# First four weight units loaded among the input chunks and split by ScalarE and VectorE, bias table's products behind them

## The chip, the cores and the metric

One core of one Trainium2 chip. The metric is the device time of one execution in microseconds (us); of the kernel before there are three runs, 3272.82 to 3274.39 us, median 3274.05. Engines in the profile: PE (TensorE matmul), PEld (its weight loads), DVE (VectorE), ACT (ScalarE), POOL (GpSimd), SP (SyncE, which here only issues DMAs).

## The reference, cut to what matters

Two stacks of two layers each run over one sequence of 512 positions with 1024 features. The change touches the first stack's first projections and a table that the second stack's attention reads much later:

```python
h = x @ w_in[l]
(fq, fk, fv, fgate, cq, ckv, kr, ...) = jnp.split(h, points, axis=-1)
log_f = jax.nn.log_sigmoid(fgate + fox_b_f[l]); cum = jnp.cumsum(log_f, axis=1)
...
q = _rmsnorm(cq, g_q) @ w_uq;  kv = _rmsnorm(ckv, g_kv) @ w_ukv;  k_rope = _rope(kr, cos, sin)
...
bias = rel_bias[t5_bucket(jnp.maximum(dist, 0))]        # second stack: (Q_BLOCK, S, 8)
logits = einsum('bqhmd,bkhmd->bhmqk', q, k) + bias
```

Everything is float32. The kernel gets float32 products from the faster fp32r matmuls by splitting every operand in a rounded part (`hi`) and the rest (`lo = x - hi`) and adding three products: hi*hi, lo*hi, hi*lo.

## The kernel before, in words

**Weights.** All weights lie in HBM as 516 units of 128 x 1024 floats (512 KB), in the order in which they are used. They pass through four slots: SP loads a unit into `raw[:, u]`, POOL makes `w_hi[:, u]` (a cast, L464) and `w_lo[:, u]` (a subtraction, L466), and PE uses it. SP may load a slot again when POOL has split what lay there (`w_split`), POOL may split into it again when PE has used it (`w_used`). A tiny add on `zero` (L463) stands at the head of every unit. Both engines run this as one loop "stream" of 129 rounds of four units. The first units are `kr` (the gate and the rotary key), `c0`, `c1` (the latent queries), `fk0`; then `c2`, `fq0`, `fq1`, `fk1`, `fv0`, `fv1`, `uq`.

**Input.** `x` comes in eight chunks of 128 x 512 (256 KB) into `resid`: even ones are issued by SP ahead of the weights (L440), odd ones by ACT (L1316). ACT makes `xn_hi` (L1093) and DVE `xn_lo` (L1509), in halves of 256 positions: first the eight first halves, then the eight second ones.

**Start of PE.** PE begins with 24 small products (L994, L995) that spread the 32 relative-position biases over distances: four score banks `bank_s` and the two `bank_a`. DVE prepares their operands (L1890 to L1902) and copies the four score banks to `t5_row` (L1912), ACT copies the other two (`copy_bank(("t5", n)...)`) and sends `t5_row` to HBM (L1333). ACT then waits for that transfer (`t5_out`, L1336) before it issues the loads of `par1`, `rope` and the `alibi` table (into `mla_v`), since `rope` and the table lie where `t5_row` lay.

**First projections.** `project_halves` runs the four first units over the chunks, half by half: `kr` and `c0` on chunk n, `c1` and `fk0` on chunk n-3 (`LN_LAG`), three matmuls of 256 columns each, 192 in all. PE reaches the first matmul of `c1` and of `fk0` at n = 3. `project` then does `c2` and `fq0` (24 matmuls of 512 columns each). After them PE waits for `added` of `("lat", "pair")`, the sum of the squares of `c0` and `c1`, and takes two token sums (L533), then `fq1`, `fk1`, the spread of the two norms (L541), and `fv` (`project_rows`), which needs both `bank_v`.

**DVE and ACT beside it.** DVE works strictly in this order: fills of `aug_q` and `aug_k` (L1917 to L1921), the wait for `rope` and the table (`par_in.after("tables1")`, L1922), the four operations that read the `kr` bank and finish the rotary key (L1926 to L1934), the copy of `fk0` (L1754), and the sum `("lat", "pair")` (L1528). ACT copies each latent bank and squares it (`latent(n)`).

Of the kernel before, what the change touches and what calls it, by code (L numbers as in the profile page):

```python
# [22 lines left out]
F32 = mybir.dt.float32  # L23
F32R = mybir.dt.float32r
ALU = mybir.AluOpType
ACT = mybir.ActivationFunctionType
# [5 lines left out]
S = 512  # L32
# [49 lines left out]
TURN_LAG = 2  # L82

# [197 lines left out]
def build(nc, t, known):  # L281
# [3 lines left out]
    with ExitStack() as ctx:  # L285
# [123 lines left out]
        act_step = signal("act_step")  # L409

# [26 lines left out]
        @block.sync  # L437
        def _(sp):
            for c in range(0, DC, 2):
                sp.dma_start(resid[:, c, :], t["x"][:, c, :]).then_inc(*x_in[c].done("x", 16))  # L440
            with loop(sp, "stream", UNITS // SLOTS) as i:
                for u in range(SLOTS):
                    sp.wait_ge(*w_split.before(("unit", u)))
                    sp.dma_start(raw[:, u, :], t["w_stream"][i, u]
                                 ).then_inc(*raw_in[u].done("unit", 16))
            for c in range(0, DC, 2):
                sp.wait_ge(*scaled.after(("final", c + 1)))
                sp.dma_start(t["out"][:, c:c + 2, :], resid[:, c:c + 2, :]).then_inc(*out_done.done(("out", c), 16))
            sp.wait_ge(*out_done.after(("out", DC - 2)))


        @block.gpsimd
        def _(pool):
            pool.sem_inc(w_split.sem, SLOTS)
            pool.memset(zero[:, :], 0.0).then_inc(*fills.done("zero"))
            pool.memset(ones[:, :], 1.0).then_inc(*fills.done("ones"))
            pool.wait_ge(*fills.after("ones"))
# [13 lines left out]
        def _(pe):  # L471
# [225 lines left out]
            def ffn_halves(tag):  # L697

                project_halves([[((tag, "gate0", k), a_bank), ((tag, "up0", k), v_bank)] for k in range(2)],
                               lambda c, s: x_lo.after(("ln2", c, s)), LN_LAG, *late_half("ln2", "layer1", DEPTH - 1))  # L700
                project((tag, "gate1", 0), a_bank)
                project((tag, "up1", 0), v_bank,
                        inside={4: lambda: square_sums("rms1", added.after(("first", DC - 1)), ln_sum[:, :])})
                project((tag, "gate1", 1), a_bank, inside={2: lambda: spread("rms1")})
                project((tag, "up1", 1), v_bank)
                ffn_rest(tag, 2)
                down(tag, None, 2)

# [278 lines left out]
            pe.wait_ge(*rel_in.after("bucket_of"))  # L987
            pe.wait_ge(*dve_step.after("rel_lo"))
            rows = slice(0, BUCKETS + 1)
            for n in range(6):  # L990
                b = bank_s[n] if n < 4 else a_bank(("t5", n))
                for m, at, cut in t5_parts(n):
                    out = b[:, at:at + cut.stop - cut.start]
                    pe.matmul(out, rel_hi[rows, m, :], bucket_r[rows, cut], start=True, stop=False)  # L994
                    mm = pe.matmul(out, rel_lo[rows, m, :], bucket_r[rows, cut], start=False, stop=True)  # L995
                mm.then_inc(*sums.done(("t5", n)))
# [88 lines left out]
        def _(act):  # L1085
# [233 lines left out]
            for s in range(2):  # L1319
                for c in range(DC):  # L1320
                    act.wait_ge(*x_in[c].after("x"))
                    split_hi_half("in1", c, s, resid[:, c, HALVES[s]])
            rows_flat = t5_row[:, :, :].rearrange("p m w -> p (m w)")
            for n in (4, 5):
                copy_bank(("t5", n), sums, rows_flat[:, n * S:(n + 1) * S])

# [4 lines left out]
            act.wait_ge(*a_read.after(("t5", 5)))  # L1331
            act.wait_ge(*dve_step.after(("t5", 3)))
            act.dma_start(t5_dram.rearrange("m q w -> q m w"), t5_row[:, :, :]).then_inc(*t5_out.done("rows", 16))  # L1333
            act.dma_start(par2[:, :], t["par2"][0]).then_inc(*par2_in.done("first", 16))
            for l in counts.laps("layer1"):
                act.wait_ge(*t5_out.after("rows"))  # L1336
                act.dma_start(par1[:, :], t["par1"][l]).then_inc(*par_in.done("par1", 16))
                act.dma_start(rope[:, :, :], t["rope"]).then_inc(*par_in.done("rope", 16))
                act.dma_start(mla_v[:, :, :], t["alibi"]).then_inc(*par_in.done("tables1", 16))
# [5 lines left out]
                latent(0)  # L1345
                latent(1)
# [7 lines left out]
                latent(2)  # L1354
# [138 lines left out]
        def _(dve):  # L1493
# [395 lines left out]
            dve.sem_inc(v_read.sem, 2)  # L1889
            dve.memset(rel_rows[BUCKETS:BUCKETS + 1, :, :], NEG)  # L1890
# [14 lines left out]
            for s in range(2):  # L1905
                for c in range(DC):
                    dve.wait_ge(*x_in[c].after("x"))
                    split_lo_half("in1", c, s)
            rows_flat = t5_row[:, :, :].rearrange("p m w -> p (m w)")
            for n in range(4):  # L1910
                dve.wait_ge(*sums.after(("t5", n)))
                dve.tensor_copy(rows_flat[:, n * S:(n + 1) * S], bank_s[n][:, :]).then_inc(*dve_step.done(("t5", n)))  # L1912
            dve.wait_ge(*act_step.after("strict_r"))

            for l in counts.laps("layer1"):
                one_hot = ident[0:4, 0:4].unsqueeze(2).to_broadcast([4, 4, S])
# [470 lines left out]
```

## Time and profile before

| | us |
|---|---|
| median of three runs | 3274.05 (3272.82 to 3274.39) |
| the profiled execution | 3273.3 |
| its span on the core | 3271.1 |
| PE busy | 3190.8 (98% of the span) |
| POOL busy | 1959.9 |
| DVE busy | 1512.6 |
| ACT busy | 710.2 |

The profile is one execution. Its span runs from the first to the last instruction; the run's own time is 2.2 us longer. The views used are the timeline (instructions of an engine by start time, equal ones merged), the waits, the windows (busy time, granted TensorE clock, GB/s by stretch) and the DMA table. An "idle" in brackets behind a row is how long that engine stood still before it, and what ended it. In merged rows the second column runs from the first start to the last end.

### The profile page before, as it was taken

What the parts mean: (1) busy time and instruction counts of PE and PEld (TensorE: products, weight loads), DVE (VectorE), ACT (ScalarE), POOL (GpSimd) and SP (SyncE); (2) the same over time, 40 slices, a digit from 0 to 9 for tenths busy, and PEclk for the clock granted to TensorE, in tenths of its full rate; (3) what the DMA queues carried; (4) which work ended last, traced back from release to release, by engine and by line L of the source; (5) the groups of instructions that cost most, each with busy time, mean ns of one, the idle gap of its engine ahead of it and who ended that gap; (6) DMA issues with size and microseconds to landing.
All of it is one profiled execution on the core that took longest, in us unless ns stands there. A gap on an engine that the chain in (4) does not pass through costs nothing.

```text
span 3271.1 us, 42400 instructions
## 1 busy us (share of the span) xinstructions
PE 3190.8 (98%) x15610; PEld 2636.1 (81%) x15610; DVE 1512.6 (46%) x1992; ACT 710.2 (22%) x1452; POOL 1959.9 (60%) x1554
## 2 busy tenths in 40 slices
PE   8999999999989999999999999999999999999998
PEld 7778888887778888878887778888888887788886
DVE  6576322265763322554317674432344237564422
ACT  2453111033532110321102231110111112321110
POOL 5334766654345666477766457776677666287763
PEclk9999999999999999999999999999999999999999
DMA  5111222222112222132223212222222232132221
GB/s 171 52 39 52 96 96 97 96 91 70 41 52 81 97 98 91 65 100 96 98 98 103 69 66 96 96 97 97 96 96 96 97 113 84 39 100 97 96 99 58
DMA packets 81417, 284.08 MB, mean 87 GB/s; under 512 B 9467, under 2 KB 12956, under 8 KB 81052
## 3 DMA queue, kind: packets, MB, share of 16 engines
q1 hardware_dynamic: 75456, 273.71, 25.1%
q10 hardware_dynamic: 5852, 8.78, 0.8%
q8 instruction: 84, 1.38, 0.2%
q14 instruction: 25, 0.20, 0.0%
HBM read 278.79 MB, written 3.67 MB: 86 GB/s over the span
## 4 chain that ended last, share of the span: by engine, by line
PE 91%; DVE 5%; ACT 1%; issue 1%; POOL 1%; DMA 0%; SPq 0%; DVEq 0%; POOLq 0%; ACTq 0%
PE bank_v L492 19%; PE bank_v L494 19%; PE bank_v L493 19%; PE bank_a L492 8%; PE bank_a L493 8%; PE bank_a L494 8%; PE bank_v L747 1%; PE bank_a L726 1%; PE bank_s L880 1%; PE bank_s L576 1%; PE bank_s L765 1%; PE bank_v L895 1%; DVE qmix L1516 0%; PE bank_a L533 0%; PE bank_s L883 0%
## 5 line engine op out<-in xcount | busy, mean ns | idle before, releaser
L466 POOL TENSOR_TENSOR w_lo<-raw,w_hi 128x1024 fp32r<-128x1024 f32 x516 | 1311.4, 2541 | 41.4
L463 POOL TENSOR_TENSOR zero<-zero 128x1 f32<-128x1 f32 x516 | 134.1, 260 | 1233.6 <-PE bank_v L494 889.3
L492 PE MATMUL bank_v<-xn_hi,w_hi 128*128 128x512 f32 (+1 forms) x1696 | 648.2, 382 | 12.2 <-DVE resid L1597 4.7
L494 PE MATMUL bank_v<-xn_hi,w_lo 128*128 128x512 f32 (+1 forms) x1696 | 639.5, 377 | 0.0
L493 PE MATMUL bank_v<-xn_lo,w_hi 128*128 128x512 f32 (+1 forms) x1696 | 639.1, 377 | 0.0
L464 POOL CAST w_hi<-raw 128x1024 fp32r<-128x1024 f32 x516 | 548.7, 1063 | 0.0
L492 PE MATMUL bank_a<-xn_hi,w_hi 128*128 128x512 f32 (+1 forms) x1248 | 477.4, 383 | 21.6 <-DVE xn_lo L1509 6.2
L493 PE MATMUL bank_a<-xn_lo,w_hi 128*128 128x512 f32 (+1 forms) x1248 | 472.6, 379 | 0.0
L494 PE MATMUL bank_a<-xn_hi,w_lo 128*128 128x512 f32 (+1 forms) x1248 | 472.4, 379 | 0.0
L492 PE MATMUL bank_v<-h_hi,w_hi 128*128 128x512 f32 (+1 forms) x1100 | 419.9, 382 | 0.0
L493 PE MATMUL bank_v<-h_lo,w_hi 128*128 128x512 f32 (+1 forms) x1100 | 418.6, 381 | 0.0
L494 PE MATMUL bank_v<-h_hi,w_lo 128*128 128x512 f32 (+1 forms) x1100 | 418.6, 381 | 0.0
L492 PEld LDWEIGHTS bank_v<-xn_hi,w_hi 128*128 128x128 f32 x1696 | 322.3, 190 | 74.2 <-issue 8.6
L494 PEld LDWEIGHTS bank_v<-xn_hi,w_lo 128*128 128x128 f32 x1696 | 321.9, 190 | 58.4
L493 PEld LDWEIGHTS bank_v<-xn_lo,w_hi 128*128 128x128 f32 x1696 | 322.3, 190 | 56.4 <-issue 1.4
L1712 DVE TENSOR_TENSOR h_lo<-work,h_hi 128x512 f32 (+1 forms) x132 | 270.0, 2046 | 119.5 <-ACT h_hi L1211 79.5
L492 PEld LDWEIGHTS bank_a<-xn_hi,w_hi 128*128 128x128 f32 x1248 | 238.5, 191 | 68.0 <-DVE xn_lo L1509 7.1
L493 PEld LDWEIGHTS bank_a<-xn_lo,w_hi 128*128 128x128 f32 x1248 | 238.8, 191 | 43.1 <-issue 1.0
L494 PEld LDWEIGHTS bank_a<-xn_hi,w_lo 128*128 128x128 f32 x1248 | 238.8, 191 | 42.7
L492 PEld LDWEIGHTS bank_v<-h_hi,w_hi 128*128 128x128 f32 x1100 | 206.8, 188 | 40.1 <-issue 0.5
L493 PEld LDWEIGHTS bank_v<-h_lo,w_hi 128*128 128x128 f32 x1100 | 206.8, 188 | 39.8 <-issue 0.5
L494 PEld LDWEIGHTS bank_v<-h_hi,w_lo 128*128 128x128 f32 x1100 | 206.8, 188 | 39.6
(355 smaller groups left out, 3367.8 us busy)
## 6 DMA issues: line engine op xcount, KB each, us to landing
raw<-in_w_stream SPq DMA_DIRECT2D x516, 512.0 KB, 3.3
rope<-in_rope ACTq DMA_DIRECT2D x2, 1024.0 KB, 5.2
da_v<-t_rows ACTq DMA_DIRECT2D x2, 1024.0 KB, 5.8
out<-resid SPq DMA_DIRECT2D x4, 512.0 KB, 2.7
t_rows<-t_row ACTq DMA_DIRECT2D x1, 1536.0 KB, 6.0
resid<-in_x SPq DMA_DIRECT2D x4, 256.0 KB, 3.6
resid<-in_x ACTq DMA_DIRECT2D x4, 256.0 KB, 9.1
mla_v<-in_alibi ACTq DMA_DIRECT2D x2, 512.0 KB, 6.2
```

Source lines behind the costliest of these rows:

```text
L463: pool.tensor_tensor(zero[:, 1:2], zero[:, 0:1], zero[:, 0:1], ALU.add)
L464: pool.tensor_copy(w_hi[:, u, :], raw[:, u, :]).then_inc(*hi_split.done(("unit", u)))
L466: pool.tensor_tensor(w_lo[:, u, :], raw[:, u, :], w_hi[:, u, :].bitcast(F32), ALU.subtract).then_inc(*w_split.done(("unit", u)))
L492: pe.matmul(out, lhs_hi, rhs_hi, start=first, stop=False)
L493: pe.matmul(out, lhs_hi, rhs_lo, start=False, stop=False)
L494: return pe.matmul(out, lhs_lo, rhs_hi, start=False, stop=last)
L576: mm = pe.matmul(column, source[:, tile], ones[:, 0:1], start=k == 0, stop=k == len(sources) - 1, skip_group_check=True)
L726: mm = pe.transpose(b[:, j * P:(j + 1) * P], source[:, j * P:(j + 1) * P], ident[:, :])
L747: mm = pe.matmul(b[half(k), i * P:(i + 1) * P], values_of(j, h), probs_t[:, k, turned_at(i) + j, :], start=(j == first_block(tag, i)), sto ...
L765: pe.matmul(b[:, 0:n], mla_q[0:96, h, cut], mla_k[0:96, h, 0:n], start=True, stop=True)
L880: pe.matmul(b[:, 0:n], mix2[half(m), h, cut], da_k[half(m), h, 0:n], start=True, stop=True)
L1712: dve.tensor_tensor(h_lo[:, at, :], work[:, 2 + k:3 + k, :], h_hi[:, at, :].bitcast(F32), ALU.subtract).then_inc(*x_lo.done((tag, h, k)))
```

## The change

SP issues the first four units and all eight chunks of `x` in one fixed order, ACT and DVE split both in the same order, and POOL's loop begins at the fifth unit. DVE's preparation of the bias operands moves behind all input splits, PE's 24 products behind `project_halves`, and ACT's two copies, the transfer of `t5_row` and `latent(2)` stand ahead of the loads of `rope` and the table.

```diff
+HEAD = (("w", 0), ("x", 0), ("w", 1), ("x", 1), ("x", 2), ("x", 3), ("w", 2), ("x", 4), ("x", 5), ("w", 3), ("x", 6), ("x", 7))
 ...
 def _(sp):
-            for c in range(0, DC, 2):
-                sp.dma_start(resid[:, c, :], t["x"][:, c, :]).then_inc(*x_in[c].done("x", 16))
-            with loop(sp, "stream", UNITS // SLOTS) as i:
+            for kind, n in HEAD:
+                if kind == "x":
+                    sp.dma_start(resid[:, n, :], t["x"][:, n, :]).then_inc(*x_in[n].done("x", 16))
+                else:
+                    sp.dma_start(raw[:, n, :], t["w_stream"][0, n]).then_inc(*raw_in[n].done("head", 16))
+            with loop(sp, "stream", UNITS // SLOTS - 1) as i:
 ...
 def _(pool):
+            w_split.done("head", SLOTS)
-            with loop(pool, "stream", UNITS // SLOTS):
+            with loop(pool, "stream", UNITS // SLOTS - 1):
 ...
 def _(pe):
-            (the 24 products, ahead of everything)
             for l in counts.laps("layer1"):
                 project_halves(...)
+                if l == 0:
+                    bias_table()
                 project(("c", 2), a_bank)
 ...
 def _(act):
+            act.wait_ge(*fills.after("zero"))
+            act.activation(small[:, 31:32], zero[:, 0:1], ACT.Copy).then_inc(*act_step.done("copy_table"))
-            for c in range(1, DC, 2):
-                act.dma_start(resid[:, c, :], t["x"][:, c, :]).then_inc(*x_in[c].done("x", 16))
+            for kind, n in HEAD:
+                if kind == "x":
+                    act.wait_ge(*x_in[n].after("x"))
+                    split_hi_half("in1", n, 0, resid[:, n, HALVES[0]])
+                else:
+                    act.wait_ge(*raw_in[n].after("head"))
+                    act.activation(w_hi[:, n, :], raw[:, n, :], ACT.Copy).then_inc(*first_hi.done(n))
 ...
+                if l == 0:
+                    act.dma_start(par1[:, :], t["par1"][l]).then_inc(*par_in.done("par1", 16))
+                    latent(0)
+                    latent(1)
+                    for n in (4, 5):
+                        copy_bank(("t5", n), sums, rows_flat[:, n * S:(n + 1) * S])
+                    act.wait_ge(*a_read.after(("t5", 5)))
+                    act.wait_ge(*dve_step.after(("t5", 3)))
+                    act.dma_start(t5_dram.rearrange("m q w -> q m w"), t5_row[:, :, :]).then_inc(*t5_out.done("rows", 16))
+                    latent(2)
+                    act.wait_ge(*t5_out.after("rows"))
                 act.dma_start(rope[:, :, :], t["rope"]).then_inc(*par_in.done("rope", 16))
                 act.dma_start(mla_v[:, :, :], t["alibi"]).then_inc(*par_in.done("tables1", 16))
 ...
 (dve)
+            for kind, n in HEAD:
+                if kind == "x":
+                    split_lo_half("in1", n, 0)
+                else:
+                    dve.wait_ge(*first_hi.after(n))
+                    dve.tensor_tensor(w_lo[:, n, :], raw[:, n, :], w_hi[:, n, :].bitcast(F32), ALU.subtract
+                                      ).then_inc(w_split.sem, 1)
+            for c in range(DC):
+                split_lo_half("in1", c, 1)
             (the bias operands, L1890 to L1902 of before)
 ...
             for l in counts.laps("layer1"):
+                if l == 0:
+                    for n in range(4):
+                        dve.wait_ge(*sums.after(("t5", n)))
+                        dve.tensor_copy(rows_flat[:, n * S:(n + 1) * S], bank_s[n][:, :]).then_inc(*dve_step.done(("t5", n)))
```

ACT's instructions before, from the copies of the two bias banks (`t_row`) to the end of the third latent (`cq`, with its square into `mla_q`); `t_rows` is the table in HBM, the first `par` is `par2`, the second `par1`:

```order
L1105 ACTIVATE t_row<-bank_a 128x512 [waits sums] x2
L1328 ACTIVATE ident_r<-ident 128x128 [waits const_in]
L1333 DMA t_rows<-t_row 128x8x384 [waits dve_step,a_read]
L1334 DMA par<-in_par 128x61
L1337 DMA par<-in_par 128x48 [waits t5_out]
L1338 DMA rope<-in_rope 128x2048
L1339 DMA mla_v<-in_alibi 128x1024
L1105 ACTIVATE cq<-bank_a 128x512 [waits w_used]
L1096 ACTIVATE mla_q<-cq 128x512 [waits a_read]
L1105 ACTIVATE cq<-bank_a 128x512 [waits w_used]
L1096 ACTIVATE mla_q<-cq 128x512 [waits a_read]
L1349 ACTIVATE work<-work 4x512 [waits dve_step]
```

And the same stretch of ACT now:

```order
L1350 DMA par<-in_par 128x48
L1115 ACTIVATE cq<-bank_a 128x512 [waits w_used]
L1106 ACTIVATE mla_q<-cq 128x512 [waits a_read]
L1115 ACTIVATE cq<-bank_a 128x512 [waits w_used]
L1106 ACTIVATE mla_q<-cq 128x512 [waits a_read]
L1115 ACTIVATE t_row<-bank_a 128x512 [waits sums] x2
L1358 DMA t_rows<-t_row 128x8x384 [waits dve_step,a_read]
L1115 ACTIVATE cq<-bank_a 128x512 [waits w_used]
L1106 ACTIVATE mla_q<-cq 128x512 [waits a_read]
L1363 DMA rope<-in_rope 128x2048 [waits t5_out]
L1364 DMA mla_v<-in_alibi 128x1024
L1370 ACTIVATE work<-work 4x512 [waits dve_step]
```

All three latents stood behind the loads of `rope` and the table, and stand ahead of them now; the transfer of the bias rows and the wait for its end moved with them, behind two of the latents.

DVE's instructions before, around the copies of the four score banks (`t_row<-bank_s`):

```order
L1509 TENSOR_TENSOR xn_lo<-resid,xn_hi 128x256 [waits x_hi,x_in7]
L1912 COPY t_row<-bank_s 128x512 [waits sums] x4
L1917 CAST aug_q<-zero 128x2048 [waits act_step]
L1918 CAST aug_k<-zero 128x512 [waits dve_step]
L1920 CAST aug_k<-ones 4x512 [waits dve_step]
L1921 CAST aug_q<-ident 4x2048
L1920 CAST aug_k<-ones 4x512
L1921 CAST aug_q<-ident 4x2048
L1926 TENSOR_SCALAR work<-bank_v,par 4x512 [waits w_used,par_in]
```

And now:

```order
L1932 CAST rel_hi<-rel_rows 33x1024
L1933 TENSOR_TENSOR rel_lo<-rel_rows,rel_hi 33x1024 [waits dve_step]
L1943 COPY t_row<-bank_s 128x512 [waits sums,act_step]
L1943 COPY t_row<-bank_s 128x512 [waits sums] x3
L1945 CAST aug_q<-zero 128x2048
L1946 CAST aug_k<-zero 128x512 [waits dve_step]
L1948 CAST aug_k<-ones 4x512 [waits dve_step]
L1949 CAST aug_q<-ident 4x2048
L1948 CAST aug_k<-ones 4x512
L1949 CAST aug_q<-ident 4x2048
L1954 TENSOR_SCALAR work<-bank_v,par 4x512 [waits w_used,par_in]
```

The order from the copies to the read of the `kr` bank is the same; what moved is that the bias operands stand ahead of them, behind the input splits, and that the products which the copies wait for come later on PE. The read of the `kr` bank still waits for `par_in`.

## Rows read from the trace of the kernel before

**Rows 1.** PE's timeline (start us, length us, what, idle before).

```profile
8.74 0.66 PE L994 MATMUL bank_s<-bucket_r,rel_hi 33*128 33x384 f32 x1 [8.74 <-DVE rel_lo L1902]
14.53 0.52 PE L995 MATMUL bank_a<-bucket_r,rel_lo 33*128 33x384 f32 x1
...
18.99 0.41 PE L493 MATMUL bank_a<-xn_lo,w_hi 128*128 128x256 f32 x1
19.20 0.41 PE L494 MATMUL bank_a<-xn_hi,w_lo 128*128 128x256 f32 x1
...
26.17 0.39 PE L492 MATMUL bank_v<-xn_hi,w_hi 128*128 128x256 f32 x1 [2.14 <-POOL w_lo L466]
...
47.30 0.28 PE L493 MATMUL bank_v<-xn_lo,w_hi 128*128 128x256 f32 x1
47.42 0.28 PE L494 MATMUL bank_v<-xn_hi,w_lo 128*128 128x256 f32 x1
48.24 0.50 PE L492 MATMUL bank_a<-xn_hi,w_hi 128*128 128x512 f32 x1 [0.54 <-POOL w_lo L466]
...
59.25 1.84 PE L533 MATMUL bank_s<-ones,mla_q 128*128 128x1 f32 x16
...
71.98 1.88 PE L541 MATMUL bank_s<-qmix,ones 128*128 128x512 f32 x4
75.55 0.36 PE L492 MATMUL bank_a<-w_hi,xn_hi 128*128 128x256 f32 x1 [1.69 <-DVE fox_k L1754]
```

**Rows 2.** POOL's timeline: start of the first unit's split, end of the fourth's.

```profile
10.26 0.42 POOL L463 TENSOR_TENSOR zero<-zero 128x1 f32<-128x1 f32 x1 [9.20 <-DMA raw<-in_w_stream]
...
23.71 2.40 POOL L466 TENSOR_TENSOR w_lo<-raw,w_hi 128x1024 fp32r<-128x1024 f32 x1
```

**Rows 3.** DVE's timeline.

```profile
7.37 1.22 DVE L1902 TENSOR_TENSOR rel_lo<-rel_rows,rel_hi 33x1024 fp32r<-33x1024 f32 x1
...
44.58 0.74 DVE L1926 TENSOR_SCALAR work<-bank_v,par 4x512 f32<-4x512 f32 x1 [9.84 <-PE bank_v L494]
...
46.79 1.94 DVE L1933 TENSOR_TENSOR work<-work 32x512 f32<-32x512 f32 x1
...
51.59 2.06 DVE L1528 TENSOR_TENSOR mla_q<-mla_q 128x512 f32<-128x512 f32 x1
...
61.87 7.52 DVE L1516 TENSOR_SCALAR qmix<-ident,small 128x128 f32<-128x128 f32 x8
```

**Rows 4.** Timeline of ACT and of the two issuing queues.

```profile
0.75 1.82 SPq L440 DMA_DIRECT2D resid<-in_x  x4
...
36.73 0.45 ACTq L1339 DMA_DIRECT2D mla_v<-in_alibi  x1
44.86 0.60 ACT L1105 ACTIVATE cq<-bank_a 128x512 f32<-128x512 f32 x1 [25.29 <-PE bank_a L494]
...
55.17 1.04 ACT L1356 ACTIVATE alibi<-mla_v 128x1024 fp32r<-128x1024 f32 x1
```

**Rows 5.** DMA table: KB each, median us from issue to landing.

```profile
raw<-in_w_stream SPq DMA_DIRECT2D x11, 512.0 KB, 3.3
t_rows<-t_row ACTq DMA_DIRECT2D x1, 1536.0 KB, 6.0
mla_v<-in_alibi ACTq DMA_DIRECT2D x1, 512.0 KB, 6.1
```

**Rows 6.** Windows: us, busy of PE, PEld, DVE, ACT, POOL, PEclk, DMA share, GB/s.

```profile
3.00:4.00 1.00, 0.00 (x0) 0.00 (x0) 0.00 (x0) 0.00 (x0) 0.00 (x0) 1.00 0.99 324
28.00:29.00 1.00, 1.00 (x7) 1.00 (x6) 1.00 (x3) 0.00 (x0) 0.00 (x0) 0.50 0.92 356
74.00:75.00 1.00, 0.00 (x0) 0.00 (x0) 0.97 (x2) 0.00 (x0) 0.92 (x2) 1.00 0.96 381
```

**Rows 7.** The input splits on DVE: shortest, median, longest ns.

```profile
L1509 DVE TENSOR_TENSOR xn_lo<-resid,xn_hi x16: 409/421/2623, 8.5 to 27.0; 128x256 fp32r<-128x256 f32 x16
```

**Rows 8.** A sum of two 128x512 tiles on DVE, whole run: busy us, mean ns.

```profile
L1528 DVE TENSOR_TENSOR fox_k<-fox_k 128x512 f32<-128x512 f32 x8 | 5.5, 684 | 0.0
```

More of the change, by code:

```diff
@@ L409, in build @@
         act_step = signal("act_step")
+        first_hi = signal("first_hi")
         v_read = signal("v_read", 2)
@@ L438, in _ @@
         def _(sp):
-            for c in range(0, DC, 2):
-                sp.dma_start(resid[:, c, :], t["x"][:, c, :]).then_inc(*x_in[c].done("x", 16))
-            with loop(sp, "stream", UNITS // SLOTS) as i:
+            for kind, n in HEAD:
[4 more added lines that the diff above has]
+            with loop(sp, "stream", UNITS // SLOTS - 1) as i:
                 for u in range(SLOTS):
                     sp.wait_ge(*w_split.before(("unit", u)))
-                    sp.dma_start(raw[:, u, :], t["w_stream"][i, u]
+                    sp.dma_start(raw[:, u, :], t["w_stream"][i + 1, u]
                                  ).then_inc(*raw_in[u].done("unit", 16))
@@ L707, in ffn_halves, with bias_table @@
                 down(tag, None, 2)
+            def bias_table():
+                pe.wait_ge(*rel_in.after("bucket_of"))
+                pe.wait_ge(*dve_step.after("rel_lo"))
+                rows = slice(0, BUCKETS + 1)
+                for n in range(6):
+                    b = bank_s[n] if n < 4 else a_bank(("t5", n))
+                    for m, at, cut in t5_parts(n):
+                        out = b[:, at:at + cut.stop - cut.start]
+                        pe.matmul(out, rel_hi[rows, m, :], bucket_r[rows, cut], start=True, stop=False)
+                        mm = pe.matmul(out, rel_lo[rows, m, :], bucket_r[rows, cut], start=False, stop=True)
+                    mm.then_inc(*sums.done(("t5", n)))
             def late_half(tag, layer, l):
@@ L986, in _ @@
             pe.wait_ge(*fills.after("ones"))
[L987 to L996, printed above, removed]
             for l in counts.laps("layer1"):
@@ L1314, in _ @@
                 act.dma_start(dest, t[name]).then_inc(*rel_in.done(name, 16))
-            for c in range(1, DC, 2):
-                act.dma_start(resid[:, c, :], t["x"][:, c, :]).then_inc(*x_in[c].done("x", 16))
             for name, dest in (("ident", ident[:, :]), ("mask", work[:, 0, 0:P]), ("strict", work[:, 0, P:2 * P])):
                 act.dma_start(dest, t[name]).then_inc(*const_in.done(name, 16))
[L1319 to L1325, printed above, removed]
+            for kind, n in HEAD:
[6 more added lines that the diff above has]
+            for c in range(DC):
+                split_hi_half("in1", c, 1, resid[:, c, HALVES[1]])
             act.wait_ge(*const_in.after("strict"))
@@ L1330, in _ @@
             act.activation(strict_r[:, :], work[:, 0, P:2 * P], ACT.Copy).then_inc(*act_step.done("strict_r"))
-            act.wait_ge(*a_read.after(("t5", 5)))
-            act.wait_ge(*dve_step.after(("t5", 3)))
-            act.dma_start(t5_dram.rearrange("m q w -> q m w"), t5_row[:, :, :]).then_inc(*t5_out.done("rows", 16))
             act.dma_start(par2[:, :], t["par2"][0]).then_inc(*par2_in.done("first", 16))
             for l in counts.laps("layer1"):
[L1336 to L1339, printed above, removed]
                 def latent(n):
@@ L1343, in latent @@
                     square(("lat", n), cq[:, n, :], mla_q[:, n, :])
-                latent(0)
-                latent(1)
+                if l == 0:
+                    act.dma_start(par1[:, :], t["par1"][l]).then_inc(*par_in.done("par1", 16))
+                    latent(0)
+                    latent(1)
+                    rows_flat = t5_row[:, :, :].rearrange("p m w -> p (m w)")
+                    for n in (4, 5):
[6 more added lines that the diff above has]
+                else:
+                    act.dma_start(par1[:, :], t["par1"][l]).then_inc(*par_in.done("par1", 16))
+                act.dma_start(rope[:, :, :], t["rope"]).then_inc(*par_in.done("rope", 16))
+                act.dma_start(mla_v[:, :, :], t["alibi"]).then_inc(*par_in.done("tables1", 16))
+                if l:
+                    latent(0)
+                    latent(1)
                 act.wait_ge(*dve_step.after("fz"))
@@ L1353, in _ @@
                 act.activation(f[:, 1, :], f[:, 1, :], ACT.Ln, bias=ones[0:4, 0:1]).then_inc(*act_step.done("f_ln"))
-                latent(2)
+                if l:
+                    latent(2)
                 act.wait_ge(*par_in.after("tables1"))
@@ L1889, in _ @@
             dve.sem_inc(v_read.sem, 2)
+            for kind, n in HEAD:
+                if kind == "x":
+                    split_lo_half("in1", n, 0)
+                else:
+                    dve.wait_ge(*first_hi.after(n))
+                    dve.tensor_tensor(w_lo[:, n, :], raw[:, n, :], w_hi[:, n, :].bitcast(F32), ALU.subtract
+                                      ).then_inc(w_split.sem, 1)
+            for c in range(DC):
+                split_lo_half("in1", c, 1)
             dve.memset(rel_rows[BUCKETS:BUCKETS + 1, :, :], NEG)
@@ L1903, in _ @@
                               ).then_inc(*dve_step.done("rel_lo"))
[L1905 to L1912, printed above, removed]
             dve.wait_ge(*act_step.after("strict_r"))
             for l in counts.laps("layer1"):
+                if l == 0:
+                    rows_flat = t5_row[:, :, :].rearrange("p m w -> p (m w)")
+                    for n in range(4):
+                        dve.wait_ge(*sums.after(("t5", n)))
+                        dve.tensor_copy(rows_flat[:, n * S:(n + 1) * S], bank_s[n][:, :]).then_inc(*dve_step.done(("t5", n)))
                 one_hot = ident[0:4, 0:4].unsqueeze(2).to_broadcast([4, 4, S])
```

## The prediction

> **What bounds the kernel now.** I read PE's share of the page first: 98% busy, so only stretches where PE stands still, or works for nothing, can give time back. The waits of PE over the whole run show one large one, 8.7 us at the start, and nothing behind the first 80 us is touched, so the timelines of those 80 us decide. [rows 1] give PE's course: bias products from 8.74 to 15.0, a few projections, a stop until 26.17, then without a break to 47.7 (47.42 + 0.28), `c2` from 48.24, token sums at 59.25, and a last stop of 1.69 us before `fv` at 75.55. The stop until 26.17 ends with POOL's split of the fourth unit [rows 2]: POOL splits from 10.26 to 26.11, 4.0 us a unit, and PE can't pass the first matmul of `fk0` without the last. So the start is bound by POOL's four splits, and before them by DMA. By 26.17 PE has done 27 of the 192 matmuls (24 of `kr` and `c0` for n = 0 to 3, three of `c1`); 165 are left.
>
> The second reading matters more here: how late DVE and ACT may be. In [rows 3] DVE reads the `kr` bank at 44.58 after standing still 9.84 us for PE, and has the sum `("lat", "pair")` at 53.65 (51.59 + 2.06), 5.6 us before PE asks for it at 59.25. The table's load is issued at 36.73 and lands 6.1 us later, at 42.8 [rows 4, 5]: DVE's wait for it is hidden by just 1.8 us.
>
> **The fourth unit, gain.** In SP's new order it ends 3.67 MB (four units of 0.52, six chunks of 0.26). A unit alone moves at 381 GB/s [rows 6], 1.4 us, and lands 3.3 us after its issue [rows 5], so 1.9 us are fixed. From SP's first issue at 0.75 [rows 4] the fourth unit lands at 0.75 + 1.9 + 3.67 MB at 324 GB/s (the rate at 3 to 4 us, [rows 6]) = 14.0, or 12.3 at 381; I take 13.6. Its `hi` on ACT costs 1.04 (the 128x1024 row at 55.17 in [rows 4]), its `lo` on DVE 1.22 (1024 elements a partition in [rows 3]). That is 15.9 against 26.17: **-10.3 us**. Bounds: 14.5 and 18. ACT and DVE keep up: DVE needs 4 x 1.22 + 8 x 0.41 = 8.2 us for all of it.
>
> I use DVE's undisturbed prices because POOL stands still there: DVE's input splits took 0.41 us at the shortest and 2.62 at the longest [rows 7], the long ones under POOL's splits. The Trainium skill (SBUF — State Buffer, Who interferes with whom) puts it as a rule: a VectorE instruction with two SBUF inputs and a GpSimd one exclude each other, and the second waits for the whole of the first. By that rule the head's splits run at the short price and DVE's work under POOL's splits at the long one; the trace agrees.
>
> Odd chunks no longer go by ACT's queue. SP's queue by itself moved 381 GB/s at 74 us, both together 324 at the start [rows 6], so I charge nothing for it.
>
> **Clock.** At 19 us matmuls of 256 columns start 0.213 us apart (1.2 GHz), at 47.3 they start 0.12 apart (2.4 GHz) [rows 1]; at 28 to 29 us the granted clock was 0.50 [rows 6], just after PE's stop. Over the stretch from 26.17 to 47.42 164 starts took 21.25 us, at 0.12 they would take 19.7: the low clock cost 1.6 us. I assume the same behind the earlier start, so `project_halves` ends 21.5 us after its fourth unit, at 37.4 (bounds 36 and 41).
>
> **Bias products, loss.** Before, 24 products took 6.3 us (8.74 to 15.05) at 1.2 GHz while PE had nothing else. Now they stand between 37.4 and `c2`: at 2.4 GHz half, 3.1 us, to 40.5. They cover the 0.54 us that PE waited for `c2`. If nothing else happened, `c2` would start at 40.5 instead of 48.24: -7.7 us.
>
> **Where it is given back.** With the products moved the chain behind them, and DVE's wait stands in it. The products end at 40.5. ACT copies the last bank, 0.6 (its copy of 128x512 in [rows 4]): 41.1; DVE's four copies are done by then. The rows' transfer takes 6.0 [rows 5]: 47.1. While it runs, SP loads units (before, POOL's slots were full and none was loaded), each 1.4 us of the DMA engines; I add 0.7: 47.8. `latent(2)`, which ACT must do first, is through at 40.5 + 5.5 (`c2`) + 1.2 = 47.2 and doesn't hold it. `rope` is issued at 47.8, the table 0.5 later, and it lands 6.1 after that [rows 5], with 0.7 for units again: 55.1. Only then can DVE read the `kr` bank. From there to the pair sum it took 9.07 us before [rows 3]. POOL will have filled its slots by about 55 (it may go on only when `fq1` is used), so the two sums of two SBUF tiles that took 1.94 and 2.06 us beside POOL [rows 3] take 0.69 each [rows 8]: 6.5 us. The pair sum is there at **61.6**, while PE, done with `c2` and `fq0` (11 us), asks for it at 51.5. PE stands still for 10 us and starts the token sums 2.4 us later than before (61.6 against 59.25). Bounds of this moment: 57 (fourth unit 1.4 us earlier, no unit beside the transfers, clock high throughout) and 66 (fourth unit 2 us later, one more unit beside each transfer).
>
> **Behind the stall.** Before, 59.25 to 75.55 took 16.3 us, of which PE waited 1.69 for DVE's `fox_k` copy, held up by eight diagonals of 0.94 us each beside POOL [rows 1, 3]. With POOL standing still these are short and the wait goes: 12.7 (token sums, `fq1`, `fk1`, from 59.25 to 71.98) + 1.9 = 14.6. But after 10 us without work PE's clock will be low, as it was at 19 us; 4 us at 1.2 GHz cost 1.9. So `fv` starts 16.5 us after the token sums, at 78.1 against 75.55: **+2.6 us**. Bounds of the clock term: 0 and 5 (11 us low, nearly all of `fq1` and `fk1`). Behind `fv` both kernels do the same, and every engine stands to PE as it stood, so the 2.6 us stay.
>
> The Trainium skill (TensorE: Matmul & The Clock Gate, Part 1) has it that the gate is throttled by default and opened by activity. By that a loss behind the stall is certain and only its size open; the trace agrees at the start, where PE, after 8.7 us without work, worked at 1.2 GHz.
>
> The rest costs nothing: ACT's early table load ends before any chunk lands; DVE's bias operands, some 4 us, end near 24, long before 37; its fills of `aug_q` and `aug_k` end before 55.
>
> **The sum.** The profiled execution took 3273.3 (span 3271.1 + 2.2), which gives 3275.9. It lies 0.75 us under the median of the runs, so for the median: 3274.05 + 2.6 = 3276.6.
>
> **Rivals.**
> A, the gain stays: PE does not stand still at the token sums, and everything behind `c2` keeps the 7.7 us. For it: the start is bound by the fourth unit, and that comes 10 us earlier. Against it: the pair sum stands behind the table's wait on an engine that works in order, and the two transfers one after the other take 12 us whatever else happens. It gives 3274.05 - 7.7 = 3266.3, and needs the chain from the products to the pair sum 10 us shorter than its rows.
> B, slower beyond doubt: the stop lowers PE's clock, and it stays low through the bias products (+3.1) and much of `fq1` and `fk1` (48 matmuls, 0.2 us dearer each, 9.7 us at most). Place: 37 to 44 and 63 to 80. It decides once PE spends more than about 12 us of both at 1.2 GHz; then the sum passes +6.5 us. For it: the clock was low at 28 us after a stop of only 2.14. Against it: dense work had raised it again well before 47. With 15 us low it costs 7 instead of 1.9: 3281.8.
> C, the head doesn't do what it says: twelve transfers on one queue run slower than 324 GB/s, or ACT, still issuing its six small loads, splits late. The fourth unit is split at 18.4 instead of 15.9. All that follows moves: 3279.1.
>
> **Chances.** The forecast 0.64, A 0.12, B 0.11, C 0.13. A change within 0.2% (6.5 us) counts as none; this is about what runs of this kernel can tell. Forecast and C lie inside it but for a tail of 1 in 100 to each side. So faster 0.13, same 0.75, slower 0.12. The forecast's own range is 3272 to 3281; stretched by the bounds towards A and B it is 3268.5 to 3282.
>
> **What would show it.** `fk0`'s first matmul at 15.9; POOL's first split near 34; `c2` near 40.5; then, and on this step all hangs, an idle time of PE of about 10 us before the token sums, with DVE standing still before its read of the `kr` bank until the table lands near 55; a granted clock of 0.50 behind it; `fv` without the 1.69 us wait. If PE's idle time there is under 3 us, I am wrong and A holds; if `fk0` starts after 18, C does.

## The result, and the profile after

The changed kernel takes 3279.76 us (median of 20 runs, 3277.12 to 3281.57), the kernel before beside it 3274.16 (20 runs, 3271.32 to 3276.97). The ratio is 1.0015, 95% interval 1.0009 to 1.0021: slower by 5 to 6 us. That is less than the 0.2% below which the prediction counts a change as none, and yet clear of zero. The profiled execution of after took 3279.81 us with a span of 3277.9, 6.8 more than before's span.

PE's timeline of the changed kernel (start us, length us, what, idle before):

```profile
16.65 0.46 PE L498 MATMUL bank_v<-xn_hi,w_hi 128*128 128x256 f32 x1 [1.90 <-DVE w_lo L1917]
...
38.12 0.44 PE L724 MATMUL bank_s<-bucket_r,rel_hi 33*128 33x384 f32 x1
...
41.78 0.52 PE L725 MATMUL bank_a<-bucket_r,rel_lo 33*128 33x384 f32 x1
42.23 0.79 PE L498 MATMUL bank_a<-xn_hi,w_hi 128*128 128x512 f32 x1
...
55.50 0.39 PE L500 MATMUL bank_a<-xn_hi,w_lo 128*128 128x512 f32 x1
63.94 3.58 PE L539 MATMUL bank_s<-ones,mla_q 128*128 128x1 f32 x16 [8.05 <-DVE mla_q L1550]
67.37 0.78 PE L498 MATMUL bank_a<-xn_hi,w_hi 128*128 128x512 f32 x1
...
80.29 1.88 PE L547 MATMUL bank_s<-qmix,ones 128*128 128x512 f32 x4
81.60 0.68 PE L498 MATMUL bank_a<-w_hi,xn_hi 128*128 128x256 f32 x1
82.12 0.28 PE L499 MATMUL bank_a<-w_lo,xn_hi 128*128 128x256 f32 x1
```

Each row has its pair in [rows 1]. The first matmul of `fk0` went from 26.17 to 16.65: the head does what it says. The token sums went from 59.25 to 63.94, behind an idle time of 8.05 us that before did not have. In both timelines the second matmul of `fv` is the safer mark, since the first one's record starts among those of the spread; it stood at 75.74 before (the row after the last of [rows 1]) and stands at 82.12. Those 6.4 us are nearly the whole difference of the spans: what lies behind 82 us adds 0.4.

PE's waits in the first 90 us of before, then of after, as a check on the whole (engine, what waited, for what: us in total, times, longest):

```profile
PE bank_s L994 <- DVE rel_lo L1902: 8.7, 1, 8.7
PE bank_a L492 <- ACT t_row L1105: 2.7, 1, 2.7
PE bank_v L492 <- POOL w_lo L466: 2.1, 1, 2.1
PE bank_a L492 <- DVE fox_k L1754: 1.7, 1, 1.7
PE bank_a L492 <- POOL w_lo L466: 0.5, 1, 0.5
```

```profile
PE bank_s L539 <- DVE mla_q L1550: 8.0, 1, 8.0
PE bank_v L498 <- DVE xn_lo L1531: 6.8, 1, 6.8
PE bank_a L498 <- DVE w_lo L1917: 2.4, 1, 2.4
PE bank_v L498 <- DVE w_lo L1917: 1.9, 1, 1.9
```

Before, PE stood still for 15.7 us in all, after for 19.1. That is 3.4 of the 6.4 us. The other 3.0 are PE working slower: counted from the distances between the starts of matmuls, against those at 2.4 GHz, before lost about 7 us to the low clock up to `fv` and after about 10. The windows show where. Windows of after (us, then busy time and instructions of PE, PEld, DVE, ACT and POOL, then PEclk, DMA share, GB/s):

```profile
35.00:40.00 5.00, 5.00 (x40) 4.87 (x39) 0.98 (x2) 2.46 (x4) 4.80 (x6) 1.00 0.05 9
40.00:45.00 5.00, 5.00 (x20) 3.98 (x19) 4.93 (x6) 1.19 (x2) 4.92 (x4) 0.57 0.61 168
45.00:50.00 5.00, 5.00 (x18) 4.00 (x17) 4.97 (x3) 0.00 (x0) 4.92 (x4) 0.75 1.03 391
...
62.00:64.00 2.00, 0.07 (x1) 0.07 (x1) 1.82 (x3) 1.98 (x4) 0.00 (x0) 0.50 0.32 129
65.00:70.00 5.00, 5.00 (x18) 4.50 (x19) 2.14 (x12) 0.32 (x2) 0.00 (x0) 0.50 0.00 0
70.00:75.00 5.00, 5.00 (x20) 3.99 (x19) 2.65 (x4) 0.00 (x0) 0.00 (x0) 0.86 0.00 0
```

There are two stretches at half clock (1.2 GHz) here. One was expected, behind the stop. The other was not: the clock falls at the end of the bias products and stays down through most of `c2`, so that `c2` and `fq0` take 13.7 us (42.23 to 55.89) instead of the 11.0 of before. The timeline shows it in the lengths: a 384-column product takes 0.33 at 39.67 and 0.52 at 41.78. (Both kernels also work at the low clock in their first products and projections; the windows give 1.00 until the clock's first recorded fall, so there one has to go by the lengths.)

DVE's timeline of after, from the copies of the score banks to the pair sum:

```profile
39.63 1.88 DVE L1943 COPY t_row<-bank_s 128x512 f32<-128x512 f32 x3
41.42 1.93 DVE L1945 CAST aug_q<-zero 128x2048 fp32r<-128x2048 f32 x1
43.38 1.27 DVE L1946 CAST aug_k<-zero 128x512 fp32r<-128x512 f32 x1
44.69 2.48 DVE L1948 CAST aug_k<-ones 4x512 fp32r<-4x512 f32 x1
...
51.83 2.10 DVE L1949 CAST aug_q<-ident 4x2048 fp32r<-4x2048 f32 x1
58.29 0.74 DVE L1954 TENSOR_SCALAR work<-bank_v,par 4x512 f32<-4x512 f32 x1 [4.36 <-DMA mla_v<-in_alibi]
...
61.22 1.22 DVE L1962 COPY mla_k<-work 32x2048 f32<-32x2048 f32 x1
...
63.19 0.69 DVE L1550 TENSOR_TENSOR mla_q<-mla_q 128x512 f32<-128x512 f32 x1
...
68.29 1.66 DVE L1538 TENSOR_SCALAR qmix<-ident,small 128x128 f32<-128x128 f32 x8
```

Against [rows 3]: the read of the `kr` bank moved from 44.58 to 58.29, and what it waits for is no longer PE but the table. Two rows are new to the argument. The fills of `aug_q` and `aug_k` now run beside POOL's splits and take 12.5 us (41.42 to 53.93); in the trace before they ran while POOL stood still, 29.72 to 34.74, 5.0 us, with the same 4x512 cast at 0.41. And the eight diagonals take 1.66 instead of 7.52; POOL stands still beside them, from 59.7 to 75.1.

ACT and its queue in after, the rows' transfer and the two loads one behind the other:

```profile
42.97 0.39 ACTq L1358 DMA_DIRECT2D t_rows<-t_row  x1
50.49 0.60 ACT L1115 ACTIVATE cq<-bank_a 128x512 f32<-128x512 f32 x1 [7.55 <-PE bank_a L500]
...
51.12 0.35 ACTq L1363 DMA_DIRECT2D rope<-in_rope  x1
51.51 0.45 ACTq L1364 DMA_DIRECT2D mla_v<-in_alibi  x1
```

The rows land 7.3 us after 42.97, at 50.3, the table 6.8 us after 51.51, at 58.3 (the DMA table of after). In [rows 4, 5] the table was issued at 36.73.

### The profile page after: what moved, and what is told of

Read it like the earlier page. It is cut to its first block, busy times and chain, and to the rows that moved or that the text cites. A ratio compares the mean times of both kernels' runs of the same rounds, so it can differ in the third digit from the quotient of the medians.

```text
span 3277.9 us, 42871 instructions
## 1 busy us (share of the span) xinstructions
PE 3196.4 (98%) x15610; PEld 2641.2 (81%) x15610; DVE 1502.2 (46%) x1996; ACT 714.8 (22%) x1457; POOL 1941.3 (59%) x1542
## 4 chain that ended last, share of the span: by engine, by line
PE 72%; issue 13%; POOL 8%; DVE 4%; ACT 1%; DMA 0%; POOLq 0%; SPq 0%; DVEq 0%; ACTq 0%
PE bank_v L498 15%; PE bank_v L500 15%; PE bank_v L499 15%; PE bank_a L498 7%; PE bank_a L499 6%; PE bank_a L500 6%; POOL w_lo L472 5%; POOL w_hi L470 3%; POOL zero L469 1%; PE bank_s L899 1%; PE bank_v L766 1%; PE bank_a L745 1%; PE bank_v L914 1%; PE bank_s L902 0%; DVE mix L2126 0%
## 5 line engine op out<-in xcount | busy, mean ns | idle before, releaser
L498 PE MATMUL bank_a<-xn_hi,w_hi 128*128 128x512 f32 (+1 forms) x1248 | 480.8, 385 | 19.1 <-DVE xn_lo L1531 6.2
```

The source lines that it names most:

```text
L498: pe.matmul(out, lhs_hi, rhs_hi, start=first, stop=False)
```

## The experiments

Each was timed beside runs of the kernel before: 3274.73 us for the first four, 3274.58 for the next three, 3274.45 for the last two. The ratios have their 95% intervals. One correction goes ahead of them. The kernel before was described here as loading `rope` and the table late because they lie where `t5_row` lay. By the offsets of the tiles they do not overlap. What does lie there is, among others, `fox_k`, into which DVE copies `fk0` behind its wait for the table. So the loads need not wait for the rows' transfer, if `t5_row` gets a place that nothing else writes that early.

### Fills first

```diff
                 (DVE, layer 0 of the first stack)
+                aug_q, aug_k fills
                 for n in range(4): wait sums ("t5", n); copy bank_s[n] to t5_row
-                aug_q, aug_k fills
```

> The changed kernel, with DVE's fills of aug_q and aug_k moved ahead of its four copies of the bias banks (into its 14.8 us of standing still). Theory: what ends last before the read of the kr bank is the landing of the table (58.3 in the changed kernel), so the pair sum stays near 63.9 and the time within 1 us of the changed kernel, about 3279 us. Rival: DVE's fills, which took 12.5 us beside POOL and ended at 53.9, set the pair sum; then it comes 4 us or more earlier and the time falls to 3275 or less.

Measured: 3280.34 us, ratio 1.0019 (1.0010 to 1.0028), the same as the changed kernel. DVE's timeline:

```profile
28.33 1.22 DVE L1944 CAST aug_q<-ident 4x2048 fp32r<-4x2048 f32 x1
37.81 2.48 DVE L1949 COPY t_row<-bank_s 128x512 f32<-128x512 f32 x4 [8.27 <-PE bank_s L725]
56.15 0.74 DVE L1954 TENSOR_SCALAR work<-bank_v,par 4x512 f32<-4x512 f32 x1 [15.86 <-DMA mla_v<-in_alibi]
```

The fills take 5.0 us again (24.52 to 29.55), and DVE gains nothing by it: it stands still for 15.86 us until the table lands. The pair sum is done at 61.7, 2.2 us before that of after, but not because of the fills: in this execution the products began at 36.98, 1.1 us earlier, and the rows left at 41.14 instead of 42.97. Behind the stop the low clock lasted longer (17.15 us from the token sums to the spread, 16.35 in after), the second matmul of `fv` starts 1.35 earlier, and over the runs nothing of it can be seen. Alone the fills are not the cause.

### Tables early

```diff
-        ..., bucket_r, t5_row = overlay(...)
+        ..., bucket_r = overlay(...)
+        _, t5_row = overlay(("before_lat", [P, 37, S], F32), ("t5_row", [P, 8, T5W], F32))
 ...
                     act.dma_start(par1 ...)
+                    act.dma_start(rope ...); act.dma_start(mla_v ..., alibi)
                     latent(0); latent(1); ... rows out ...; latent(2)
-                    act.wait_ge(*t5_out.after("rows"))
-                act.dma_start(rope ...); act.dma_start(mla_v ..., alibi)
 ...
+                if l == 0: act.wait_ge(*t5_out.after("rows"))   (behind the copy of fq1)
```

> The changed kernel, with rope and the alibi table loaded at about 16 us, ahead of the bias rows, and the bias rows kept in another place (where the latents' parts go later), so that nobody waits for their transfer. Theory: DVE then goes on at 53.9, when its fills end, instead of 58.3, with POOL still busy beside it: pair sum near 61.5, and 2 to 3 us off the changed kernel: about 3277. Rival, the table's wait alone is the stall: PE no longer waits for the pair sum, 8 us of stall and 3 us of low clock go: about 3269.

Measured: 3278.93 us, ratio 1.0009 (1.0000 to 1.0018).

```profile
52.28 2.10 DVE L1953 CAST aug_q<-ident 4x2048 fp32r<-4x2048 f32 x1
54.39 0.74 DVE L1958 TENSOR_SCALAR work<-bank_v,par 4x512 f32<-4x512 f32 x1
...
57.32 1.94 DVE L1966 COPY mla_k<-work 32x2048 f32<-32x2048 f32 x1
...
60.01 2.00 DVE L1554 TENSOR_TENSOR mla_q<-mla_q 128x512 f32<-128x512 f32 x1
```

DVE no longer waits for the table, it comes to the `kr` bank straight from the fills, at 54.39. So there are two causes side by side, either of which alone holds the pair sum past 61 (61.7 in "fills first", 62.0 here): the table's landing, and the fills at the price they have beside POOL's splits. The 3.9 us that the earlier read gained shrank to 1.9 at the pair sum, because the work behind it now runs beside POOL too (1.94 and 2.00 for 1.22 and 0.69).

### Both

The two edits above together.

> Both edits: fills ahead of the copies, tables loaded early. Theory: the pair sum is there near 50, before PE asks for it at 55.7; the stall of 8.0 us and the low clock behind it (3.4 us) go, the 1.7 us wait for fox_k may come back: about 3279.8 - 8.0 - 3.4 + 1.7 = 3270 us, 4 us below the kernel before. Rival, something else gives the time back behind the stall: 3274 or more.

Measured: **3265.65 us** (7 runs, 3263.28 to 3270.30), ratio 0.9969 (0.9958 to 0.9980): better than both kernels, and 4 us better than expected (the 1.7 us wait for `fox_k` did not come back, and the clock stayed up in the products and in `c2`). DVE, then PE:

```profile
41.35 0.73 DVE L1958 TENSOR_SCALAR work<-bank_v,par 4x512 f32<-4x512 f32 x1
...
49.30 2.07 DVE L1554 TENSOR_TENSOR mla_q<-mla_q 128x512 f32<-128x512 f32 x1
```

```profile
41.28 0.34 PE L726 MATMUL bank_a<-bucket_r,rel_lo 33*128 33x384 f32 x1
...
52.83 1.84 PE L540 MATMUL bank_s<-ones,mla_q 128*128 128x1 f32 x16
...
65.56 1.88 PE L548 MATMUL bank_s<-qmix,ones 128*128 128x512 f32 x4
```

The pair sum is there at 51.4, before PE asks, and neither a stop nor a wait for `fox_k` is left. PE's waits of the first 90 us sum to 11.3 (6.8, 2.3, 2.0 and 0.2), 4.4 less than before. The second matmul of `fv` stands at 67.39, 8.4 before the kernel before's; the other 4 us are the products, which took 3.5 us at the full clock (38.12 to 41.62, against 6.3), and the clock in the first projections. This shows that the moved products can keep the head's gain, and that it was these two causes together that took it.

### Pair sum first

```diff
+                if l == 0: wait squared ("lat", 1); add_pair(("lat", "pair"), ...)
                 dve.wait_ge(*par_in.after("tables1"))
 ...
-                wait squared ("lat", 1); add_pair(("lat", "pair"), ...)
+                if l: wait squared ("lat", 1); add_pair(("lat", "pair"), ...)
```

> The changed kernel, with one DVE instruction moved in the first layer: the sum of the two squares (lat, pair) stands ahead of DVE's wait for the table. Theory, it is DVE's strict order that hands the table's lateness to PE: the pair sum is there at 54.6 to 56, PE asks at 55.7, so the stall goes although the table lands as late as ever (58.3): about 3271 us. Rival, PE would only wait elsewhere (for the kr bank before fk1, or for the diagonals): 3276 or more.

Measured: 3271.09 us (11 runs, 3270.31 to 3277.24), ratio 0.9990 (0.9981 to 0.9999). The token sums start at 57.08 behind 0.92 us of idle. This kernel keeps the table's wait and the slow fills and only frees PE from them, and its median is 8.7 us under that of the changed one. Its runs fall in two groups, eight from 3270.31 to 3273.07 and three from 3276.49 to 3277.24, and the profiled execution (3276.66) is one of the three. In it a later wait comes up, since DVE is still late by the table; PE's timeline:

```profile
57.08 1.95 PE L539 MATMUL bank_s<-ones,mla_q 128*128 128x1 f32 x16 [0.92 <-DVE mla_q L1550]
...
75.90 0.55 PE L498 MATMUL bank_a<-w_hi,xn_hi 128*128 128x256 f32 x1 [4.13 <-DVE fox_k L1776]
```

Behind this wait the granted clock is 0.50 from 76 to 80 us. Whether the eight faster runs had the wait, no trace shows.

### Extra matmuls in the stop

```diff
                 (PE, between fq0 and the wait for the pair sum)
+                if l == 0:
+                    pe.wait_ge(*dve_step.after(("t5", 3)))
+                    for _ in range(32):
+                        pe.matmul(bank_s[2][:, :], xn_hi[:, 0, 0:P], xn_hi[:, 0, :], start=True, stop=True, ...)
```

> The changed kernel, with 32 extra matmuls of 512 columns on PE ahead of its wait for the pair sum, into a score bank that nobody reads (7.3 us, the length of the stall). Theory: behind the stall PE works at 1.2 GHz; the token sums took 3.43 us instead of 1.7, and 9 matmuls of fq1 0.427 apart instead of 0.227: with the extra work the clock stays up and 3.4 us go: about 3276.4. Rival: the low clock costs nothing or doesn't come from the stall: 3279 to 3280, more if the extra work is in the way.

Measured: 3277.57 us (3273.28 to 3284.68), ratio 1.0010 (1.0001 to 1.0019). PE behind the stop:

```profile
62.53 1.95 PE L539 MATMUL bank_s<-ones,mla_q 128*128 128x1 f32 x16 [0.70 <-DVE mla_q L1555]
64.33 0.48 PE L498 MATMUL bank_a<-xn_hi,w_hi 128*128 128x512 f32 x1
```

The matmuls ran from 54.41 to 61.82, and from 55 to 75 us the granted clock is 1.00. From the token sums to the spread it took 12.8 us (62.53 to 75.33), in after 16.35 (63.94 to 80.29). So the low clock behind the stop costs 3.5 us in the trace. (The token sums came 1.4 us earlier because the products did, 36.84 against 38.12.) The medians lie 2.2 us apart, with runs scattered over 11 us, and the intervals of the two ratios overlap: over the runs the gain is not clear of noise.

### The move without the head, and the head without the move

```diff
  (move alone: SP, POOL, ACT and DVE begin as before)
-            for kind, n in HEAD: ...
+            for c in range(0, DC, 2): sp.dma_start(resid[:, c, :] ...)
  (head alone: operands and products as before, PE begins with them)
+            bias_table()
             for l in counts.laps("layer1"):
                 project_halves(...)
-                if l == 0:
-                    bias_table()
```

> One part of the change alone: the bias products, their copies, the rows' transfer and the table loads behind the first four units as in the changed kernel, but the units loaded and split by POOL and the inputs loaded as in the kernel before. Theory: everything behind the four units comes as late against them as in the changed kernel, and they end 9.5 us later (47.7 instead of 38.1): about 3279.8 + 9.5 = 3289 us. Rival, the moved chain is hidden when the units come late: below 3280.

> The other part alone: units loaded and split among the inputs as in the changed kernel, but bias operands, products, copies, transfer and table loads first as in the kernel before. Theory: PE does the products to 15 us, the 27 matmuls to about 20, the other 165 by about 41, c2 starts near 42 instead of 48.2, the table lands near 37 and DVE waits for nothing: 3274.7 - 6.5 = about 3268 us. Rival, that the products in front cost what the early units give: 3273 or more.

Measured: move alone 3290.26 us (5 runs, 3289.39 to 3294.53), ratio 1.0050 (1.0036 to 1.0064); head alone 3270.61 (3268.00 to 3274.41), ratio 0.9987 (0.9978 to 0.9996). Against 3274.58 that is +15.7 and -4.0. In the move alone PE stands still for 9.89 us before the token sums, at 75.32. In the head alone there is no such stop (56.80). But its bias operands come late; DVE's timeline:

```profile
8.34 0.15 DVE L1906 TENSOR_TENSOR rel<-rel,rel_far 32x8 f32<-32x8 f32 x1 [6.31 <-DMA bucket_of<-in_bucket_of]
...
10.23 1.22 DVE L1915 TENSOR_TENSOR rel_lo<-rel_rows,rel_hi 33x1024 fp32r<-33x1024 f32 x1
```

`rel_lo` starts at 10.23 instead of 7.37 [rows 3], behind a small load that lands later among the weight units. The products start at 11.60 instead of 8.74. In this trace `fv` starts 2.5 us earlier than before, where 5.4 were to be had without that delay; so the late load can account for most of what is missing from the 6 expected, though no run takes it away. The profiled execution (3274.41) is the slowest of the eleven, and its span, 3272.6, is 1.5 longer than that of before: behind `fv` it lost 4 us, and the cause of that is open. The move is what costs. The two parts do not add up: +15.7 and -4.0 make +11.7, and together they gave +5.6. With the products moved the head is worth 10 us, since all that follows is tied to the fourth unit; with the products first it is worth 4.

### Products over 128 rows

```diff
+            (POOL, at its start: zero casts into all of rel_hi, rel_lo and bucket_r)
-                rows = slice(0, BUCKETS + 1)
+                rows = slice(0, P)      (PE's operands of the 24 products)
```

The first of the two is the changed kernel with this edit, the second "both" with it.

> The changed kernel, but the 24 bias products contract 128 rows instead of 33, the added ones zero (POOL fills the three operands with zeros while it has nothing to do at the start). In the profile of the changed kernel the granted clock fell to half during these products, at about 40.7 us, and stayed low until about 47.5, so that c2 began and ended late. Theory (the products that use 33 of the 128 rows let the clock fall): the windows from 40 to 50 us show 1.00, c2 ends near 48 instead of 50.4, ACT is not held by the third latent, the table lands about 2 us earlier, and the median is 3277.5. Rival (the fall has nothing to do with the rows; it comes in some executions and not in others): the median stays 3279 to 3280 and the low clock shows there again as often as before. Price of the extra rows themselves: none is expected, a matmul's length went by its columns.

> Fills first and tables early together (which took 3265.65, from 3263.28 to 3270.30), and the bias products with 128 rows as well. Here the pair sum is no longer late, so low-clock time in c2 and fq0 would go straight into the end. Theory (33-row products let the clock fall in some executions): the slow executions near 3270 vanish, median 3264.5 and all within 3262.5 to 3267. Rival (the scatter comes from elsewhere): median 3265.7 with the same spread of 7 us.

Measured: 3280.05 us (11 runs, 3278.27 to 3283.65), ratio 1.0018 (1.0009 to 1.0027); and 3264.60 (6 runs, 3262.26 to 3267.20), ratio 0.9968 (0.9956 to 0.9980). The extra rows cost nothing that can be seen. ACT's queue in the first, then PE:

```profile
40.70 0.39 ACTq L1361 DMA_DIRECT2D t_rows<-t_row  x1
...
50.33 0.37 ACTq L1366 DMA_DIRECT2D rope<-in_rope  x1
```

```profile
63.58 3.57 PE L542 MATMUL bank_s<-ones,mla_q 128*128 128x1 f32 x16 [12.19 <-DVE mla_q L1553]
```

The clock stayed at 1.00 from 35 to 50 us, and the third latent was copied at 45.99 instead of 50.49. Yet the time is the rival's. The rows left 2.3 us earlier (1.5 of them because the products began at 36.65 in this execution, which is not the edit's doing) and took 9.6 us instead of 7.3, so that they land at 50.3 as before, and DVE reads the `kr` bank at 57.94 against 58.29. PE, done with `fq0` at 51.4 instead of 55.9, stood still for 12.19 us instead of 8.05: the stop took back what the clock gave. So what the low clock cost PE in `c2` was hidden by the stop. What it cost the chain (0.6 us in the products, 0.8 by the third latent, in the trace of after) these two traces do not tell, for the longer transfer covers it. Why the rows took 2.3 us longer is not shown: in both traces two weight units are issued beside them, and the DMA engines are about as busy (share 1.02 and 1.07 in the windows of 44 to 46 and 46 to 48 us, in after 0.92 and 1.06). In "fills first" the rows left at 41.14 and took 7.4.

Whether the 33 rows let the clock fall is not settled. It fell in the profiles of after, "pair sum first" and "extra matmuls" within the products, in those of "fills first" and of the move alone between their end and the first matmul of `c2`; it stayed up in those of "tables early" and "both", with 33 rows, and in the two with 128. The second kernel's spread is 5 us instead of 7, too few runs to tell the two apart.

## Why the prediction was right, and where it was off, point by point

It said 3276.6, range 3268.5 to 3282, no change within 0.2%, and it measured 3279.76: inside the range, and slower by 5.6 us where 2.6 were forecast. In part it was luck: of two things that it did not foresee, the dear fills ended inside the wait for the table and moved nothing in this kernel, and the time that the low clock cost PE in `c2` was taken up by the stop.

**The fourth unit: right, 0.7 us late.** 16.65 against 15.9; `project_halves` took the 21.5 us expected of it (16.65 to 38.12).

**The bias products: the price was too low.** They took 4.1 us (38.12 to 42.23) instead of 3.1: at the full clock they take 3.5 ("both"), and here the clock fell in their last quarter. The step "at 2.4 GHz half" had no bound for that. On PE the difference vanished in the stop; on the chain it made the rows leave 1.0 us later.

**The chain to the pair sum: right in kind, 2.3 us late.** Predicted 61.6, it is done at 63.88. By terms: the rows issued at 42.97 instead of 41.1 (+1.9); their transfer 7.3 instead of 6.7 (+0.6), with two units beside it and not half of one; ACT held by the third latent (+0.8), which the prediction said would not hold it, because `c2` took 8.1 us at the low clock and not 5.5; the two loads 7.2 instead of 7.3 (-0.1); DVE's read of the `kr` bank and the six operations behind it 5.6 instead of 6.5 (-0.9), since POOL had stopped as argued and the copy into `mla_k` fell from 2.08 to 1.22 as well. The idle time of PE, 8.05 where about 10 were predicted, is shorter although the chain is later: PE asked at 55.9 and not at 51.5, 0.7 of it by the fourth unit, 1.0 by the products and 2.6 by the low clock in `c2`.

**The fills: a cause that was missed.** The prediction placed their end "before 55", and 53.93 is so, but saw no price in it. "Tables early" shows that without the table's wait they would have held the pair sum to 62.0 by themselves. The rule cited from the Trainium skill (SBUF — State Buffer, Who interferes with whom) is about two inputs in SBUF, and the fills have one. But the prediction's own rows had the sign: the diagonals, which multiply one tile by a scalar, took 0.94 each beside POOL [rows 3]. The same section also says that copies, casts and tensor_scalar operations can take the port that VectorE shares with GpSimd, when they run in a mode that uses two ports. The prediction did not weigh that sentence. The trace agrees that such operations are held up: the 4x512 cast takes 2.48 us beside POOL for 0.41 alone, the diagonals 7.52 in [rows 3] for 1.66. In which mode they ran it does not show.

**Behind the stop: the step that was mis-sized.** The prediction charged 16.5 us from the token sums to `fv` (12.7 and 1.9 of low clock, and 1.9 of spread). Measured to the second matmul, 0.2 behind the first in before, it is 18.2. The wait for `fox_k` did go, and the clock was low, but for 7.4 us (63.94 to 71.36) where 4 were assumed, and the sixteen token sums of one column took twice as long as well (3.43 from the first start to that of `fq1`, against 1.70 in [rows 1]). The term is about 3.5 us, not 1.9; "extra matmuls in the stop" shows it in its trace by taking it away.

**Rivals.** A failed by its own condition: PE stood still 8.05 us, and 3 was the mark. But its time, 3266.3, is what "both" reached (3265.65): it needed "the chain 10 us shorter", and got it by moving a load and six fills. That the two times are so near is partly chance: `c2` began 6.4 us earlier there (41.83) and not 7.7, and the wait for `fox_k` went too, which A had kept. C did not happen. B is the nearest to what was missed: the clock was low both in the products and behind the stop, some 14 us in all (about 40.7 to 47.5 and 63.9 to 71.4), but the first half of it lay in front of the stop, where PE lost nothing by it and the chain at most the 1.4 us named above. B's term of 7 us would have needed both to be on the path.

For the profiled execution the prediction gave 3275.9, and it took 3279.81, 3.9 us more; the traces account for 2.3 at the pair sum and 1.5 behind it. For the median the difference is 3.2, because the prediction added 0.75 us by which the profile of before lay under its median, while that of after lies at its own (3279.76).

## What to carry to other kernels

When work is moved behind the thing it used to overlap, follow what waited for its result through every in-order engine to the next point where the bound engine waits: here 10 us gained at the start came out as +5.6, because a table load and six fills that had been hidden before stood one behind the other in DVE's order. Two causes side by side each look harmless when removed alone (both single edits were worth 1 us or nothing, together 14); take both away before giving up a change. And ask of every vector instruction whether the move puts it beside GpSimd's work or away from it.

## What the runs showed of the hardware

- Casts on DVE with one input in SBUF suffered beside GpSimd's splits as two-input sums did: 5.0 us of fills became 12.5. The copy of a PSUM bank into `fox_k` took 0.69 us in both company and alone.
- In three of the seven profiles with the products of 33 rows behind the projections, the granted clock fell to half in the last of them, with no wait of PE in the trace (0.57 in the window of 40 to 45 us in after, 1.00 in the same window of "both"), and in two more right behind them. With 128 rows both profiles had 1.00. Cause open.
- Matmuls of one column took twice the time at the low clock too: sixteen in 3.58 us (1.84 at full clock).
- A transfer that leaves earlier need not land earlier: 1536 KB took 6.0 us with no weight units beside it [rows 5], 7.3 issued at 42.97 beside two, and 9.6 issued at 40.70 beside as many; over the kernels with weight units beside it 7.3 to 9.6.
- Small loads of ACT's queue landed later when SP's queue began with weight units: DVE could use `bucket_of` at 8.34 us in the head alone and at 5.48 in before, issued at 1.86 and 1.80.
